# Projections and convolution of the later 512 tokens moved from the mixer into the gathers' part

## The reference

```
proj = rms_norm(h) @ w_in                         # q, k, v (512 each), gate inputs ga, gg (512 each)
attn = softmax(q1 k1 - alibi) - lam softmax(q2 k2 - alibi), times v      # 4 heads, causal
u    = ga * sigmoid(gg)
conv = silu(group_norm(depthwise_conv31(u) + b))  # causal: a token needs the 30 before it
h    = h + concat(attn, conv) @ w_out
q    = rms_norm(h) @ wq                           # 8 heads x 256
for each token and head: top 16 of 128 x 128 product keys -> 16 expert rows e, gate = softmax
h    = h + sum_k gate_k * gelu(u_tab[e_k] . x) * v_tab[e_k]
out  = rms_norm(h)[16:]
```

## Time and profile before

| | us |
|---|---|
| three runs | 3079.91, 3081.67, 3081.95 (median 3081.67) |
| profiled execution | 3080.33, its span 3078.6 |
| PE / DVE / ACT / POOL busy | 2300.7 / 2071.3 / 1328.8 / 1162.7 |
| granted TensorE clock, mean | 0.856 |
| DMA moved | 1139.68 MB, 370 GB/s in the mean |
| first gather issued | 461.64 |

### The profile page before, as it was taken

One profiled execution on the slowest core, in us unless ns is written; L12 is line 12 of the kernel. 1 busy time (PEld: TensorE's weight loads), 2 busy tenths in 40 slices (PEclk: granted clock), 3 DMA queues, 4 the chain that ended last, 5 costly groups with the idle time before them and its releaser, 6 DMA issues.

```text
span 3078.6 us, 35490 instructions
## 1 busy us (share of the span) xinstructions
PE 2300.7 (75%) x11776; PEld 848.3 (28%) x11776; DVE 2071.3 (67%) x4903; ACT 1328.8 (43%) x3979; POOL 1162.7 (38%) x1077
## 2 busy tenths in 40 slices
PE   9998857778677777777677777777777777777665
PEld 5555532222222222222222222222222222222211
DVE  3997426666677777777666666666666667666664
ACT  1023523444355555455544444444444444444443
POOL 1001004444354444445444344434444344444442
PEclk9999978898889898889898789878887788887886
DMA  5002139999999999999999999999999999999997
GB/s 215 21 28 73 58 125 415 426 426 427 426 422 426 412 424 416 420 415 426 427 421 426 426 427 426 426 427 423 422 426 425 424 423 425 427 427 421 424 426 310
DMA packets 165608, 1139.68 MB, mean 370 GB/s; under 512 B 18608, under 2 KB 21040, under 8 KB 32688
## 3 DMA queue, kind: packets, MB, share of 16 engines
q0 software_dynamic: 150096, 1082.80, 83.9%
q1 hardware_dynamic: 15328, 54.62, 4.6%
HBM read 1122.06 MB, written 15.28 MB: 369 GB/s over the span
## 4 chain that ended last, share of the span: by engine, by line
DMA 43%; PE 23%; ACT 10%; DVE 6%; issue 3%; POOL 1%; SPq 0%; DVEq 0%; POOLq 0%; ACTq 0%
DMA ring<-table,e_odd 21%; DMA ring<-table,e_even 20%; PE acc L1623 14%; PE qq_ps L1597 5%; DVE ring L1426 4%; ACT diag L1191 2%; ACT weight L1184 2%; ACT L1258 2%; ACT L1177 1%; PE proj L1570 1%; ACT gelu L1258 1%; ACT wide L1215 1%; PE acc L1661 1%; DVE wide L1441 1%; PE s_ps L1614 1%
## 5 line engine op out<-in xcount | busy, mean ns | idle before, releaser
L1623 PE MATMUL acc<-ring,diag 64*64 64x512 f32 x8192 | 1327.4, 734 | 695.0 <-ACT diag L1191 693.3
L1426 DVE CUSTOM_DVE_ANT_0 ring<-ring,xn_odd 128x1024 f32<-128x1024 f32 x512 | 626.7, 1224 | 366.8 <-DMA ring<-table,e_even 183.2
L1040 POOL DMA_INDIRECT ring<-table,e_even x512 | 567.2, 1108 | 791.2 <-PE acc L1623 700.9
L1426 DVE CUSTOM_DVE_ANT_0 ring<-ring,xn_even 128x1024 f32<-128x1024 f32 x512 | 626.4, 1223 | 337.7 <-DMA ring<-table,e_odd 168.7
L1040 POOL DMA_INDIRECT ring<-table,e_odd x512 | 568.1, 1110 | 706.7 <-PE acc L1623 665.3
L1258 ACT ACTIVATE gelu<-dots 128x1 f32<-128x1 f32 x1024 | 205.5, 201 | 1197.0 <-DVE dots L1426 1195.2
L1623 PEld LDWEIGHTS acc<-ring,diag 64*64 64x64 f32 x8192 | 250.0, 150 | 1469.2 <-ACT diag L1191 1342.0
L1191 ACT ACTIVATE diag<-pairs,weight 128x64 f32<-128x64 f32 x1024 | 356.0, 348 | 33.6
L1597 PE MATMUL qq_ps<-wq_rest,xnT_cur 128*128 128x256 f32 x896 | 262.6, 430 | 0.0
L1597 PEld LDWEIGHTS qq_ps<-wq_rest,xnT_cur 128*128 128x128 f32 x896 | 173.1, 209 | 174.1 <-issue 154.0
L1184 ACT ACTIVATE weight<-gelu,gate_even 128x1 f32<-128x1 f32 x512 | 150.7, 294 | 16.7
(11 more groups left out here) (237 smaller groups left out, 2106.3 us busy)
## 6 DMA issues: line engine op xcount, KB each, us to landing
ring<-table,e_even POOLq DMA_INDIRECT x512, 15.1
ring<-table,e_odd POOLq DMA_INDIRECT x512, 15.1
wq_rest<-wq SPq DMA_DIRECT2D x7, 1024.0 KB, 13.0
w_own<-w_units SPq DMA_DIRECT2D x10, 512.0 KB, 3.4
xT<-xt SPq DMA_DIRECT2D x8, 520.0 KB, 7.6
h_next<-x SPq DMA_DIRECT2D x8, 512.0 KB, 8.1
wide<-w_out SPq DMA_DIRECT2D x2, 2048.0 KB, 8.5
wide<-w_out SPq DMA_DIRECT2D x1, 4096.0 KB, 17.5
```

What stands on the lines that cost most here:

```text
L1040: pool.indirect_dma_start(out=ring[:, g % RING, :], out_offset=None, in_=table[:, :], in_offset=bass.IndirectOffsetOnAxis(ap=e_row[m % 2][ ...
L1426: dve.tensor_tensor_reduce(ring[:, g % RING, 0:D], ring[:, g % RING, 0:D], xn[(m // PH) % 2][:], 1.0, 0.0, ALU.mult, ALU.add, dots[:, k:k ...
L1623: ins = pe.matmul(acc[ACC_OF[t]][ROWS[j], HALF[i]], diag[ROWS[i], g % DIAGS, :], ring[ROWS[i], g % RING, D + j * 512:D + (j + 1) * 512], s ...
```

## The change

The mixer now handles only the meta tokens and tokens 0 to 511 (`FRONT` = 528 columns); the projections and the convolution of tokens 512 to 1023 (`BACK` = 512) are done in the expert part.

- Mixer: `xT`, `kT_all`, `q_all`, `u_pad`, `y` are half as wide; a unit has two segments of 264; V has five groups (meta and four tiles); a tap covers 512 tokens. The later tokens are loaded into `x2`, their squares summed after A of group 0 (`mean_squares(8..15)`), and DVE normalises them in place (`normalise_late`, within the taps of group 1). `x2` stays for the expert part. The last 30 columns of each `u_pad` go to DRAM (`keep_tail`). Fillers: eight instead of fifteen; K of head 2 comes before the loop.
- Expert part: 20 *jobs* (K, G, A, Q, V by head or group), one per frame from frame -7 to 12, where frames now start at gather 174 (`FRAME0`, two steps later than before). A job's weights, 512 KB, are loaded into `w_job` as soon as the job before has been multiplied; PE does its eight blocks two by two in slots 4 to 7 of a step; ACT copies the result in slot 10 (DVE multiplies it in slot 12 for A); SP stores K, Q and V to DRAM. After each A job follow on DVE 31 taps, one per slot, then centring, a reciprocal in four parts and a multiplication, with means and variances on PE and squares, roots and Silu on ACT.
- Of the heads of wq only five later ones have a place from the start; four heads share two of the places and are loaded anew: six loads (`next_pair`) and two into `x2` after the last job (`wq_last`).
- The output projections of tiles 1 to 3 are done in the order 2, 3, 1 in other slots (`SLOTS`), that of tile 4 in slots 449 to 458; `begin(1)` stands at the start of tile 1.
- `normalise(0)` waits for g2 alone (`b_g2`); `gf_half` has its own semaphore, waited for in the first `last_scale`.

```diff
-SEGS = [(0, 352), (352, 352), (704, 336)]
+FRONT = META + P * EARLY
+BACK = P * LATE
+SEGS = [(0, FRONT // 2), (FRONT // 2, FRONT // 2)]
...
-FRAME0 = (1 * PH + 0) * TOPK + 14
+FRAME0 = (1 * PH + 2) * TOPK + 14
+FIRST_JOB = -7
+JOBS = [K[0], G[0], A[0], Q[0], V[0], K[1], G[1], A[1], Q[1], V[1], K[2], G[2], A[2], Q[2], V[2], K[3], Q[3], V[3], G[3],
+        A[3]]
+PIECES = {6: (0, 1), 7: (2, 3), 8: (4, 5), 9: (6, 7)}
+ORDER = [2, 3, 1, 4, 5, 6, 7]
+SLOTS = {2: (3, 5, 7, 9, 11, 13, 15, 19), 3: (25, 27, 29, 31, 35, 37, 39, 41), 1: (47, 51, 52, 53, 55, 56, 57, 59)}
+SLOTS[4] = tuple((3 * PH + 4) * TOPK + k for k in (1, 2, 3, 5, 7, 8, 9, 10))
...
             gated(1)
-            taps(1, 0, 20)
-            centre(0, 0)
-            centre(0, 1)
-            taps(1, 20, TAPS)
+            taps(1, 0, 8)
+            normalise_late()
+            centre(0)
+            taps(1, 8, 16)
             divide(0)
+            taps(1, 16, TAPS)
...
-            for j in (G[0], A[0], G[1], A[1]):
-                for n in range(3):
+            for j in (G[0], A[0]):
+                for n in range(2):
                     seg(j, n)
-            for m in range(5):
+            for k in range(KC, 2 * KC):
+                mean_squares(k)
+            for j in (G[1], A[1]):
+                for n in range(2):
+                    seg(j, n)
+            for m in range(EARLY + 1):
                 values(m)
...
+            def job_weights(n):
+                sp.wait_ge(j_pe, n)
+                sp.dma_start(w_job, w_units[JOBS[n]]).then_inc(j_w, 16)
...
+                if f == UNITS:
+                    sp.wait_ge(c_st, 16 * CG)
+                    sp.wait_ge(t_pv, UNITS)
+                    sp.wait_ge(t_o, UNITS)
+                    sp.dma_start(w_out_s, w_out).then_inc(b_w2, 16)
...
+            def job_out(n):
+                j = JOBS[n]
+                act.wait_ge(j_pe, n + 1)
+                src = job_banks(FIRST_JOB + n)
+                if j in G:
+                    if j > G[0]:
+                        act.wait_ge(c_st, 16 * (j - G[0]))
+                    act.activation(u_back[:, TAIL:], src, ACT.Sigmoid).then_inc(j_ev, 1)
+                else:
+                    if KEPT.index(j) >= 1:
+                        act.wait_ge(j_st, 16 * KEPT.index(j))
+                    act.activation(kept[:], src, ACT.Copy).then_inc(j_ev, 1)
...
+            def tap(c, i):
+                if i == 0:
+                    dve.wait_ge(j_ev, JOBS.index(A[c]) + 1)
+                    dve.wait_ge(c_in, 32 * (c + 1))
+                    dve.tensor_scalar(y[:], u_back[:, 0:BACK], cpar[:, 0:1], cpar[:, TAPS:TAPS + 1], ALU.mult,
+                                      ALU.add).then_inc(c_dve, 1)
+                else:
+                    dve.wait_ge(c_dve, C_DVE * c + i)
+                    dve.scalar_tensor_tensor(out=y[:], in0=u_back[:, i:i + BACK], scalar=cpar[:, i:i + 1], in1=y[:],
+                                             op0=ALU.mult, op1=ALU.add).then_inc(c_dve, 1)
...
-            dve.wait_ge(b_par, 48)
+            dve.wait_ge(b_g2, 16)
             normalise(0)
...
+            def job_piece(n, k):
+                j, f = JOBS[n], FIRST_JOB + n
+                if k == 0:
+                    pe.wait_ge(j_w, 16 * (n + 1))
+                    if n >= 1:
+                        pe.wait_ge(j_ev, n)
+                    if 0 <= f < UNITS:
+                        pe.wait_ge(t_z, sc_at[f + 1])
+                    elif FRAME0 + TOPK * f + 6 >= PH * TOPK:
+                        pe.wait_ge(b_acc, 2)
+                if j in V:
+                    t = k // 2
+                    for i in range(4 * (k % 2), 4 * (k % 2) + 4):
+                        ins = pe.matmul(job_banks(f)[:, t * P:(t + 1) * P], x2[:, i, t * P:(t + 1) * P], w_job[:, i, :],
+                                        start=(i == 0), stop=(i == KC - 1))
+                else:
+                    ins = pe.matmul(job_banks(f), w_job[:, k, :], x2[:, k, :], start=(k == 0), stop=(k == KC - 1))
+                if k == KC - 1:
+                    ins.then_inc(j_pe, 1)
```

More of the change, by code:

```diff
@@ L582, in _ @@
             dve.tensor_scalar(sub_gain[:], par[:, KC:KC + 1], 1.0 - LAM_INIT, None, ALU.mult).then_inc(p_lam, 1)
-            dve.wait_ge(p_lamv, 16)
+            dve.wait_ge(p_std, 2)
+            dve.reciprocal(rstd[:, 0:FRONT], rstd[:, 0:FRONT]).then_inc(p_rstd, 1)
+            dve.wait_ge(p_rstd, 1)
+            for n in range(2):
+                raw_keys(0, n)
+            for k in range(KC):
+                normalise(k)
+            for n in range(2):
+                raw_keys(1, n)
+            dve.wait_ge(p_par, 32)
             for n in range(2):
@@ L923, in expert_phase @@
         sc_ps = [acc[0][:, 0:512], acc[0][:, 512:D]]
+        mean_ps = acc[0][:, 512:D]
         b_const = sem("b_const")
-        b_par = sem("b_par")
-        b_wq = [sem(f"b_wq{h}") for h in range(PH)]
+        b_g2 = sem("b_g2")
+        b_gf = sem("b_gf")
+        b_wq = [sem(f"b_wq{h}") for h in range(1, PH)]
         b_w2 = sem("b_w2")
@@ L1102, in _ @@
             tokens(3)
+            next_pair(0, 0)
+            sp.wait_ge(b_op, 3)
+            mix(1)
+            put_aside(3)
+            tokens(1)
+            next_pair(0, 1)
             sp.wait_ge(b_op, 4)
+            job_weights(0)
             sp.dma_start(bias, dram["bias"]).then_inc(t_bias, 16)
-            keys_and_queries(0)
-            values(0)
-            put_aside(3)
-            fetch(2)
-            store(0)
-            keys_and_queries(1)
-            values(1)
-            keep_head(0)
@@ L1749, in _ @@
                             output(u, 1)
+                    if o in PIECES and 0 <= u - FIRST_JOB < len(JOBS):
+                        for piece in PIECES[o]:
+                            job_piece(u - FIRST_JOB, piece)
+                    c, at = conv_at(m, k)
+                    if at == 38:
+                        group_means(c)
+                    elif at == 41:
+                        group_variances(c)
                     if t >= 1 and h == 1 and k == 3:
```

726 lines of the change are left out of this document (446 added, 280 removed).

## The result

| | before | after |
|---|---|---|
| median of 4 runs, us | 3081.40 (3079.91 to 3081.95) | 3052.74 (3048.28 to 3053.20) |
| profiled execution, us (span) | 3080.33 (3078.6) | 3048.28 (3046.5) |
| granted TensorE clock, mean | 0.856 | 0.853 |

The ratio is 0.9903, 95% interval 0.9889 to 0.9918: faster by 29 us, where 71 were forecast. The sign, the bytes and the gf_half wait came as predicted; what the engines lose among the gathers was far too small in the sum.

A forecast was written before the change was run, and what follows sets the result against it. TensorE and VectorE were taken to bound the 416 us mixer, bytes the 1024 gathers. 3080.3 - 83 - 35 - 20 + 57 + 12 = 3011, forecast 3010; its own range 2992 to 3030, the wider range 2970 to 3060.

The forecast's parts named there:

- Part 1: Mixer up to its unit loop: narrower work brings the first unit's scores at 172 against 254.75, -83 us.
- 70 taps 54.4, two divisions 8, ...: Mixer, VectorE's path after the first group mean: taps, divisions, centrings, gatings, mean and a root wait, 70.5 us in all.
- Part 2: The mixer's unit loop and end: fewer and narrower fillers and shorter units, -35 us (bounds -45 and -14).
- rival (b): Mixer's unit loop falls to 1.2 GHz, so the second half takes 58 instead of 41 us: 3040, chance 0.08.
- 33, 4 and 3: Second half of the unit loop: 33 us for the units' chain, 4 for the last division, 3 for table loads.
- Part 3: Between mixer and gathers: normalise(0) no longer waits for gf_half, so the first gather starts earlier, -20 us.
- Part 4: Among the gathers: 23.1 MB of added loads and stores cost their bytes, +57 us.
- Part 5: Engines among the gathers: jobs and taps make some frames late, but rows in flight hide most, +12 us (bounds 0; 60).
- (a): Among the gathers: engines set the pace in job frames and the ring hides nothing, 3059 (half of it 3035), chance 0.19.
- (d): Among the gathers: TensorE at a low granted clock in job frames, slower than before, 3175 at 0.65, chance 0.04.
- the 7 us: Among the gathers: what VectorE's taps were forecast to cost after most of their lateness is hidden.
- if TensorE's clock there is below 0.78: Job frames among the gathers: a sign that would show the forecast wrong.

The follow-up runs named there:

- e18: Changed kernel with ScalarE's last activation of channel group 1 ahead of the evictions of queries 0 and keys 2 in its queue: 3047.0 us.
- e4: Kernel before, with only the first normalisation waiting for g2 alone and the wait for g_final's halves moved to their first use: 3062.0 us.
- e8: Changed kernel with 6 of a job's 8 matmuls left out and 30 of 31 taps on 8 columns (results wrong): 3014.9 us.
- e1: Changed kernel with 6 of each job's 8 matmuls left out, loads, stores, taps and evictions kept (job results wrong): 3015.6 us.
- e17: Changed kernel with two more matmuls per job in frame slot 6, their result overwritten, the job's own eight still two by two in slots 6 to 9: 3040.2 us.
- e12: Changed kernel with three matmuls over 264 columns, whose result nobody reads, in each of the mixer's attention units 8 to 14: 3045.1 us.

## Why the prediction was wrong

**Part 1, the mixer up to the unit loop: the path right, one wait missed.** The wait for the first group mean was forecast at 16 and is 17.0 us, and moving it gave 10.7. The result is -75.4 instead of -83. The step that failed is the list "70 taps 54.4, two divisions 8, ...": it has no wait for the store of channel group 1, which ACT's queue delays. e18 gives 5.4 of the 7.4 us. (The wait for the first root, 3.3 in the sum, is 2.7.)

**Part 2, the unit loop: -30.2 instead of -35.** Units 0 to 7 and the end came as forecast (58.9 and 25.2 us for 60 and 25). Units 8 to 15 took 47.2 instead of 41, at a clock of 0.55: rival (b) happened, in half of the loop and at a smaller price. The Trainium skill, "TensorE: Matmul & The Clock Gate", Part 1, calls the throttled state the default that activity releases; the trace agrees, since the clock was 0.95 for the units with fillers, 0.55 for those without, and 0.92 with three idle-filling matmuls. The rival's price was too high: with the clock up again only 2.9 of the 6.2 us came back, so the loop hangs on something else more than on PE's speed, by the prediction's own account on the chain through DVE and ACT. The other 3.3 us are open; the forecast's terms (33, 4 and 3) add up to 40, not 41, which makes them one more.

**Part 3: -19.7 instead of -20** (from the mixer's end to the first gather 45.5 us before, 25.8 after), shown alone by e4.

**Part 4: right, as far as shown.** 57 us forecast; 58.2 by e8, which has all the bytes and loads but a quarter of the matmuls; what that quarter costs is in the 58.2 and not known.

**Part 5: the step that failed.** It said: "35.4 to 38 of 41.1" for TensorE, "43.9 to 45.8" for VectorE in six frames, and "Eight rows in flight hide 6 to 10 us. So most of it is hidden", +12 us. It was 34.9 (2710.1 - 2675.2), of which 29.6 lie in the 13 frames with a job and a unit. TensorE's sum over a frame was right (606 us in 760 are 36.7 in a frame of 46.1) and the wrong measure. Inside the frame the job's 7.5 us lie in four slots; with the gathers' four times 1.09 and the routing's 1.1 that is 13 us of work in 9.8 us of slots, around a stand of 4.5 us that the sum didn't hold at all and of which the first pair fills only 1.9. Why the ring's eight rows did not hide it, as the 6 to 10 us in the sum had it, no run shows; that the attention unit's stand had used up this slack already would fit, since the kernel before, with the same stand, still moved 421 GB/s. VectorE's sum, on which the 7 us rested, was the lesser matter: beside e1's edit shorter taps gave nothing measurable, alone 11 us.

**The rivals.** (a), 3059, was nearest to 3052.7, with 0.19. Its price for jobs, 30 us, is about right. Its mechanism, jobs that hold up the scores, is only the last link: VectorE's wait for scores did grow, from 75.8 us, which is also the value of 840 to 1600, to this (changed kernel, 860 to 1620, as long a stretch):

```profile
DVE wide L1619 <- PE acc L1888: 91.8, 31, 7.2
```

But what came late first was PE, behind ACT's exponentials. Of (d) the mechanism was there, small: a low clock right behind the stand, not in the mean, where 0.91 from 860 to 1620 hid it, and the kernel before had it too. My condition "if TensorE's clock there is below 0.78" looked at a mean and could not have found it; "if windows in the job frames fall below 400" did.

**The miss of 43 us** is 12.8 of the time before the first gather, 24.1 of the part behind it, and 5.8 of which 4.5 are that the profiled execution lies so far below the median of the four runs, where I had taken the median near it, and 1.3 that the sum gives 3011.3 and the forecast was set at 3010. The result lies between the forecast and rival (a), nearer to the rival: Parts 1 to 4 hold in the main, Part 5 does not.

## What to carry to other kernels

Work that is to hide beside a pipeline has to fit slot by slot, not on the average of a period: list for the few slots it goes into what the engine does there and how long it stands for others, and put it into the stand, not behind it. A stand is the one place where the engine's time is free, and filling it kept TensorE's clock up here for what follows. A low clock that costs little in the kernel as it is can cost much once work is put behind it. Where the rate of a stream falls while every engine has room, look on the timeline for what frees the stream's buffers, and for the wait ahead of it.

## What the runs showed of the hardware

- Adding work made the kernel faster: two matmuls of 0.94 us in a stand of 4.5 us, whose result is overwritten, took 12.5 us off (e17). Right behind the stand of frame 9 the gathers' four matmuls took 1.98 instead of 1.09 us in the changed kernel, and in the kernel before as well.
- The same stretch of the mixer ran at a granted clock of 0.55, with TensorE busy for 34.26 of 47.21 us, and at 0.92, busy for 32.06 of 44.35, with three more matmuls in seven of its eight units (e12).
- Bytes are not worth their size where engines hold a stream up: 16.1 MB less gave 17 us, not 38 (e3), and only 3.6 of them in the 13 frames that the engines held up.
